# A mixture-of-experts stage on one core: expert places of 64 seats, and places that alternate 64 and 32 seats

## What is computed

```python
def moe_ffn(h, w_router, b_router, w_gu, b_gu, w_down, b_down):
    logits = jnp.matmul(h, w_router, preferred_element_type=F32) + b_router
    top_val, top_e = lax.top_k(logits, TOP_K)
    gates = jax.nn.softmax(top_val, axis=-1)
    ...
    def expert_block(a):
        xi, e = a
        gate, up = jnp.split(xi @ w_gu[e] + b_gu[e], 2, axis=-1)
        gate = jnp.minimum(gate, SWIGLU_LIMIT)
        up = jnp.clip(up, -SWIGLU_LIMIT, SWIGLU_LIMIT)
        act = (up + 1.0) * gate * jax.nn.sigmoid(SWIGLU_ALPHA * gate)
        return act @ w_down[e] + b_down[e]
```

## Time and profile before

| | us |
|---|---|
| median of 3 runs | 1625.09 |
| lowest, highest run | 1615.44, 1627.84 |
| span of the profiled execution | 1618.4 |
| the stage of experts in it | from 500.5 to 1595.2 |
| mean granted TensorE clock, share of full | 0.966 |

### The profile page before, as it was taken

The page is one execution under the profiler, slowest core; times in us unless marked ns, Lnnn a source line. Parts: engine busy times, 40 slices in busy tenths (PEclk is TensorE's granted clock), DMA queues, the critical chain, the costliest instruction groups (busy, mean ns, idle before and its releaser), DMA issues.

```text
span 1618.4 us, 24363 instructions
## 1 busy us (share of the span) xinstructions
PE 1467.1 (91%) x8993; PEld 741.2 (46%) x8994; DVE 397.1 (25%) x762; ACT 261.4 (16%) x530; POOL 203.1 (13%) x426
## 2 busy tenths in 40 slices
PE   7998789998877999999799899979989998999995
PEld 6786556776543334344234343424434443334331
DVE  1134443223435112112112111211211121122115
ACT  1234441212132111101000010100001010001002
POOL 2000010000113111112111121111112111111101
PEclk9999899999997999999999899989999998999998
DMA  8316286334965999995899899589999957999970
GB/s 268 130 56 222 93 295 203 104 131 169 332 274 226 383 408 404 414 379 222 323 415 416 351 397 376 210 314 412 417 362 399 385 208 314 409 417 405 370 298 30
DMA packets 117232, 483.21 MB, mean 299 GB/s; under 512 B 7963, under 2 KB 40899, under 8 KB 84099
## 3 DMA queue, kind: packets, MB, share of 16 engines
q1 hardware_dynamic: 115378, 475.36, 75.0%
q0 software_dynamic: 1664, 5.53, 1.0%
q10 hardware_dynamic: 48, 0.13, 0.0%
HBM read 475.35 MB, written 5.64 MB: 297 GB/s over the span
## 4 chain that ended last, share of the span: by engine, by line
PE 88%; issue 6%; DVE 4%; ACT 2%; DMA 1%; POOL 0%; SPq 0%; DVEq 0%; ACTq 0%; POOLq 0%; PEldq 0%
PE bank L997 31%; PE bank L1024 15%; PE bank L508 12%; PE bank L955 8%; PE bank L967 5%; PE bank L517 4%; PE bank L498 3%; PE bank L958 2%; PE bank L990 1%; PE bank L1008 1%; PE bank L822 1%; PE bank L1012 1%; ACT area L1351 1%; PE bank L681 1%; PE bank L656 1%
## 5 line engine op out<-in xcount | busy, mean ns | idle before, releaser
L997 PE MATMUL bank<-ring,area 128*64 128x512 f32 x1728 | 393.4, 609 | 4.4 <-issue 4.3
L997 PEld LDWEIGHTS bank<-ring,area 128*64 128x64 f32 x1728 | 134.6, 141 | 248.5 <-issue 242.5
L2209 DVE TENSOR_SCALAR area<-bank 128x512 f32<-128x512 f32 x35 | 24.2, 692 | 886.6 <-PE bank L997 886.6
L1351 ACT ACTIVATE area<-bank 64x288 f32<-64x288 f32 (+6 forms) x268 | 134.6, 523 | 503.6 <-PE bank L1024 227.9
L1024 PE MATMUL bank<-ring,area 128*64 128x512 f32 x768 | 170.1, 595 | 0.0
L508 PE MATMUL bank<-ring 128*128 128x288 f32 x640 | 160.3, 408 | 6.1 <-PE bank L508 4.2
L508 PEld LDWEIGHTS bank<-ring 128*128 128x128 f32 x640 | 120.3, 190 | 44.2 <-issue 10.1
L955 PE MATMUL bank<-area 128*128 128x512 f32 x288 | 133.2, 605 | 0.8 <-ACT area L1351 0.8
L1692 ACT ACTIVATE area<-area 128x512 f32<-128x512 f32 x35 | 22.0, 630 | 579.9 <-DVE area L2209 579.9
L997 PE MATMUL bank<-area 128*64 128x512 f32 x512 | 115.6, 599 | 0.0
L2196 DVE TENSOR_TENSOR area<-area,bank 128x512 f32<-128x512 f32 (+1 forms) x180 | 110.4, 678 | 9.3 <-PE bank L955 9.2
(11 more groups left out here) (208 smaller groups left out, 1043.4 us busy)
## 6 DMA issues: line engine op xcount, KB each, us to landing
ring<-in_w_gu SPq DMA_DIRECT2D x192, 1024.0 KB, 8.8
ring<-in_w_down SPq DMA_DIRECT2D x96, 1024.0 KB, 11.8
area<-in_w_gu SPq DMA_DIRECT2D x64, 1024.0 KB, 9.6
area<-in_w_down SPq DMA_DIRECT2D x32, 1024.0 KB, 14.6
ring<-in_w_in SPq DMA_DIRECT2D x12, 1024.0 KB, 9.6
ring<-in_w_mkv SPq DMA_DIRECT2D x8, 1024.0 KB, 10.4
ring<-in_cache_k SPq DMA_DIRECT2D x16, 512.0 KB, 5.0
ring<-in_cache_v SPq DMA_DIRECT2D x16, 512.0 KB, 5.5
```

What stands on the lines that cost most here:

```text
L997: last = pe.matmul(bank[1 + j][64 * h:64 * h + 64, :], xgT[:, k, :], w[:, D * j + 512 * h:D * j + 512 * h + 512], start=False, stop=(k == ...
L1351: return act.activation(out, in_, ACT.Copy, scale=scale)
```

## The change

`KINDS` gives the places the kinds 64, 32, 64, 32 and so on; a further block always has 32 seats.

- *Narrow blocks.* A block of 32 seats uses `xgT[:, k, 0:32]` as the stationary operand and four column tiles of 32, each with 256 of the weights' 1024 columns. The activations then fill 256 columns of a bank and not 512, so DVE's and ACT's instructions are half as wide and two transposes do. The product with `w_down` puts its two row blocks r into tiles of their own (rows 64h + 32r), so that `y_s` holds two partial sums, which the combining product adds because the selection (`slot4`) repeats each seat.
- *Combining product.* `selT` is one 128 x 256 matrix and each half is a matmul over 64 rows, `selT[64h:64h+64]` times `y_s[64h:64h+64]`, so that two *row tiles* stand where there was a full-height matmul with zeros. The 32 sample tokens keep the full height (`sel_end`).
- *Counts and order.* The 28 experts are sorted by token count; the 14 with most go to the wide places, the 14 with fewest to the narrow ones. The number of further blocks is worked out for either kind (`more_wide`, `more_narrow`).
- On ACT, DVE and POOL the loops over places become loops over pairs.

```diff
+KINDS = (64, 32, 64, 32)
+FURTHER = 32
...
-    first = [3, 11, 19, 7, 15, 0, 5, 9, 13]
-    places = first + [i for i in range(NE - GROUP) if i not in first]
+    wide = [i for i in range(NE - GROUP) if KINDS[i % GROUP] == CAP]
+    narrow = [i for i in range(NE - GROUP) if KINDS[i % GROUP] != CAP]
+    places = wide[3::4] + wide[2::4] + wide[1::4] + wide[0::4] + narrow[0::2] + narrow[1::2][::-1]
...
-                        pe.matmul(bank[COMB_BANK[2 * c + h]][:, :], selT[h][:, P * c:P * c + P], y_s[:, :],
+                        rows = slice(64 * h, 64 * h + 64)
+                        pe.matmul(bank[COMB_BANK[2 * c + h]][:, :], selT[rows, P * c:P * c + P], y_s[rows, :],
                                   start=True, stop=True).then_inc(comb, 1)
...
-            def expert_block(group, q, release, last_block=False):
+            def expert_block(group, q, release, kind, last_block=False):
+                parts, width = P // kind, D * kind // P
...
-                        for h in range(2):
-                            last = pe.matmul(bank[1 + j][64 * h:64 * h + 64, :], xgT[:, k, :], w[:, D * j + 512 * h:D * j + 512 * h + 512],
-                                             start=False, stop=(k == KB - 1))
+                        for t in range(parts):
+                            last = pe.matmul(bank[1 + j][kind * t:kind * t + kind, 0:width], xgT[:, k, 0:kind],
+                                             w[:, D * j + width * t:D * j + width * t + width], start=False, stop=(k == KB - 1))
...
-                for j in range(4):
+                for j in range(width // P):
...
+                            else:
+                                at = 64 * h + 32 * r
+                                last = pe.matmul(bank[4][at:at + 32, :], actT[:, r, 32 * i:32 * i + 32],
+                                                 w[:, r, 512 * h:512 * h + 512], start=(i == 0), stop=(i == 3))
...
                 with pe.If(more > 0):
                     with pe.Fori(0, more):
-                        expert_block(group, q, False)
+                        expert_block(group, q, False, FURTHER)
...
-                copy(selT[0][0:64, :], bank[5][0:64, 0:T])
-                copy(selT[1][64:128, :], bank[5][64:128, 0:T]).then_inc(selT_ready, 1)
+                copy(selT, bank[5][:, 0:NPT])
+                for h in range(2):
+                    last = copy(sel_end[64 * h:64 * h + 64, h, :], bank[5][64 * h:64 * h + 64, NPT:T])
...
+            step(dve.tensor_tensor(beyond, halves_of.unsqueeze(2).broadcast_to([1, NE, MORE_MAX]),
+                                   C("iota", 1, 1 + MORE_MAX, 1).unsqueeze(1).broadcast_to([1, NE, MORE_MAX]), ALU.is_gt))
...
-            counts = nxf[0:1, GROUP:NE]
+            counts = tokens_of[0:1, GROUP:NE]
```

More of the change, by code:

```diff
@@ L1251, in _ @@
                 pool.dma_start(y_s[64 * h:64 * h + NE, :], A["b_down"][0][:, 512 * h:512 * h + 512]).then_inc(late_in, 16)
-            for i in range(2):
-                clear(selT[i])
+            clear(selT)
+            clear(sel_end)
             clear(topf, -1.0)
@@ L1308, in expert_block, with expert @@
                 pool.reg_add(blocks_done, blocks_done, 1)
-            def expert(e, counts, at):
-                more = pool.value_load(counts[0:1, bass.ds(at, 1)], min_val=0, max_val=4)
+            def expert(e, counts, at, kind):
+                more = pool.value_load(counts[0:1, bass.ds(at, 1)], min_val=0, max_val=MORE_MAX)
                 with pool.If(more > 0):
                     with pool.Fori(0, more) as i:
[L1314 to L1318, removed]
+                        expert_block(e, FURTHER, i * FURTHER + kind)
+                expert_block(e, kind, None)
+            with pool.Fori(0, GROUP // 2) as pair:
+                for i in range(2):
+                    expert(pair * 2 + i, nextra, pair * 2 + i, KINDS[i])
             pool.wait_ge(order_ready, 1)
-            with pool.Fori(GROUP, NE) as at:
-                expert(pool.value_load(order[0:1, bass.ds(at, 1)], min_val=0, max_val=NE - 1), nextra_at, at)
+            with pool.Fori(GROUP // 2, NE // 2) as pair:
+                for i in range(2):
+                    at = pair * 2 + i
+                    expert(pool.value_load(order[0:1, bass.ds(at, 1)], min_val=0, max_val=NE - 1), nextra_at, at, KINDS[i])
             pool.wait_ge(ln3_in, 32)
@@ L2175, in _ @@
             dve.wait_ge(tokens_ready, 4)
[L2176 to L2181, removed]
+            step(dve.tensor_tensor(who_s, cmp_s, across(ids), ALU.mult))
+            settle()
+            step(dve.tensor_reduce(val, who_s, AX, ALU.add))
+            settle()
+            step(copy(order[0:1, GROUP:NE], val))
+            by_kind = [t.rearrange("p (a b) c -> p a b c", b=2) for t in (who_s, cmp_s)]
+            for b, more in ((0, more_wide), (1, more_narrow)):
+                step(dve.tensor_tensor(by_kind[0][:, :, b], by_kind[1][:, :, b],
+                                       more[0:1, GROUP:NE].unsqueeze(1).broadcast_to([1, REST // 2, REST]), ALU.mult))
+            settle()
+            step(dve.tensor_reduce(val, who_s, AX, ALU.add))
+            settle()
+            step(copy(nextra_at[0:1, GROUP:NE], val))
             settle()
```

120 lines of the change are left out of this document (69 added, 51 removed).

## The result

The changed kernel took 1551.4 us (median of 4 runs, 1550.0 to 1554.8) beside 1622.4 for the kernel before: a ratio of 0.957 [0.954, 0.959]. Forecast were 1498 us and a range of 1465 to 1550: the direction was right, of the 127 us forecast 71 came.

A forecast was written before the change was run, and what follows sets the result against it. Weight supply was to replace PE (880 us) as the bound: 388.8 MB at 413 GB/s, 941 us from 506, plus 22 us of full slots; last product at 1470, then 22.5 us: span 1492, median 1498, range 1465 to 1550.

The forecast's parts named there:

- The blocks: PE's ledger in the stage of experts: 16 wide blocks of 27.7 us and 21 narrow ones of 17.0, together 800 us.
- The supply: Loading of expert weights: 388.8 MB at 413 GB/s take 941 us, over PE's 880, so it becomes the bound.
- 22 us of full slots: Time in which no weight slot is free: 7 us in places 0 to 4, 5 at each of three further blocks.
- The gaps: Gaps and slow starts on PE in the stage of experts: 80 us, kept unchanged for the changed kernel.
- The clock falls where PE waits for weights: Rival, chance 0.20: in 21 narrow blocks, 6 us after the combining product take 12; PE needs 1006 us, median 1537.
- The 0.66 of the earlier trace: Granted clock in 5 us of the earlier trace's first part, with PE busy for 3.19; cited for the clock rival.
- The supply doesn't keep its rate: Rival, chance 0.06: weights in the stage come at 367 GB/s, 388.8 MB take 1059 us, median 1617, no change.
- The tiles don't overlap: Rival, chance 0.04: small tiles in the stage's blocks don't run side by side; narrow block 28.7 us, 1677, slower.
- The signs named: For right: stage at 400 GB/s or more, share near 1, PE busy some 200 us less, waits in narrow `w_gu` products.

The follow-up runs named there:

- kernel without jumps: The changed kernel with PE's code for further blocks kept only at places needing it on this input, 24 of 32 conditions taken out: 1486.7 us, ratio 0.917.
- full-height run: The changed kernel with the full-height combining product of the kernel before, selT in two buffers, instead of row tiles: 1614.4 us.

## Why the prediction was right and wrong

**The blocks: right.** Wide 27.7 us, measured 27.7; narrow 17.0, measured 16.57; row tiles two at a time, measured 1.91 for 3.63 (forecast 1.82); 37 blocks, as 2664 records of the gathering product show.

**The supply: right, but not yet the bound.** The sum gave 969.5 us for the stage at 413 GB/s with 22 us of full slots. The last product was to end at 1470; in the kernel without jumps it ended at 1461.9, at 408 GB/s and a full share, 1487 us in all. The Trainium skill (DMA: Bandwidth & Descriptors, section Specifications) gives about 358 GB/s for a core. The 408 GB/s over 920 us are again above it.

**The gaps: the step that failed.** "I keep all 80 for the changed kernel: its loop on PE still has four places to a turn." They became 1023.9 - 791 = 233 us, and by that PE stayed the bound: 880 us were forecast for it, under the supply's 941, and 1024 came. The step read the earlier trace rows as the price of a turn, and a turn hadn't changed. In fact most of each piece came only with the jump over the further block's copy at the first place after the turn, and the change makes this copy longer at every place (further blocks have 32 seats, and so twice the matmuls with the weights). The five pieces at turns grew from 41 to 56 us; more came elsewhere: PE's waits at other places and inside the products grew from 22 to 117 us, and slow work from 18 to 60. The diff shows the longer copy; the ledger counted what PE runs and left out what it jumps over.

**The rivals.** *The clock falls where PE waits for weights* (1537) was the nearest in us, but for another reason: PE waited for instructions, and the clock fell after that. In the kernel that does wait for weights, three of the four waits shown above are followed by a chunk in 1.07 us and only the last by one in 1.93. The combining product behind that one took 3.79 us for 1.99, but over 2.5 us in only five of this run's 38, and in none of the kernel after: what the rival put at 6 us for each of 21 blocks came seldom. The Trainium skill (TensorE: Matmul & The Clock Gate, section HAM oscillation — how this bites in real kernels) describes a matmul kernel whose clock goes back at every wait on DMA between its bursts. Here, at waits of 1.4 us that are shorter than in that kernel, it seldom did. The 0.66 of the earlier trace rows came with a longer wait, and not for DMA: within those 5 us PE resumed after 2.30 us for ACT. *The supply doesn't keep its rate* looked right at 379 GB/s; the 63 us of the full-height run and the 65 of the run without jumps show that the low rate came from PE, which didn't free the slots. The sign named for this rival, a full share at under 380 GB/s, was all but there (0.95 and 379), and misled. *The tiles don't overlap* is refuted by the block's rows.

**The signs named.** A stage at 400 GB/s with a full share, and waits for weights inside the product with `w_gu`, were to show the forecast right. After had neither, though PE's busy time fell by 186 us, near the 200 named; the kernel without the jumps had both.

## What to carry to other kernels

Rarely used code that stands in the main path can have a price that grows with its length, even if it is never run; when such a copy grows, look at the waits for "issue" first. Count what an engine jumps over as well as what it runs, and put the rare case behind one condition for several places. And measure a part's worth with the next bound in view: the row tiles were worth 63 us beside the jumps here, and 11 without them.

## What the runs showed of the hardware

- A never-taken condition over one register instruction added nothing measurable to the time (24 of them, 1554.7 beside 1551.4 us); over a block's code it cost 6.7 us, with two loads of 16 KB on the queue of instructions. No row names these loads as a releaser, but all 39 waits of over 1 us in the kernel after end 1.2 to 1.8 us behind one. Not settled is why a copy that is 72 matmuls longer turns jumps without a wait into waits of about 2 us at most places.
- After such a wait the same work is slow: four records of the bias product took 1.07 us after 11.08 of waiting, and 0.60 in a place without a wait.
- Pairs of 64-row tiles ran side by side: 1.91 us for eight records with 512 columns, where eight of full height took 3.63.
